# The low half of the MLP weights: ScalarE's negated copy and two adding transfers in place of GpSimd's subtraction

## The reference, cut to what matters

```
def _sqrelu_mlp(h, w1, w2):
    u = jax.nn.relu(h @ w1)
    return (u * u) @ w2

def second_block(...):
    for i in range(DEPTH_2):
        hn = _rmsnorm(h, mix_norm_g[i])
        ...
        h = h + _sqrelu_mlp(_rmsnorm(h, mlp_norm_g[i]), mlp_w1[i], mlp_w2[i])
    return _rmsnorm(h, final_norm_g)
```

## Time and profile before

| | us |
|---|---|
| median of the 2 runs shown | 1996.18 (1995.83 to 1996.54) |
| span of the profiled execution, first to last instruction | 1992.5 |
| PE busy in it | 1975.0 |
| GpSimd busy in it | 915.7 |
| ScalarE busy in it | 782.6 |
| VectorE busy in it | 974.1 |

### The profile page before, as it was taken

The page is one execution under the profiler, slowest core; times in us unless marked ns, Lnnn a source line. Parts: engine busy times, 40 slices in busy tenths (PEclk is TensorE's granted clock), DMA queues, the critical chain, the costliest instruction groups (busy, mean ns, idle before and its releaser), DMA issues.

```text
span 1992.5 us, 24116 instructions
## 1 busy us (share of the span) xinstructions
PE 1975.0 (99%) x9360; PEld 1640.7 (82%) x9360; DVE 974.1 (49%) x1447; ACT 782.6 (39%) x1137; POOL 915.7 (46%) x662
## 2 busy tenths in 40 slices
PE   8999999999999999999999999999999999999998
PEld 7877878888888888888888888888888888888887
DVE  7667753432358745454555131325466783132234
ACT  7546442321235443434354132233455553223232
POOL 2433555545455344444445454545333345454552
PEclk9999999999999999999999999999999999999999
DMA  5312367375322313232323323233222223323231
GB/s 162 93 49 69 116 94 123 88 101 114 100 90 85 127 64 106 65 104 68 101 66 103 100 90 106 84 105 105 84 84 85 94 74 106 106 85 105 92 98 64
DMA packets 165555, 187.05 MB, mean 94 GB/s; under 512 B 3992, under 2 KB 152224, under 8 KB 165344
## 3 DMA queue, kind: packets, MB, share of 16 engines
q1 hardware_dynamic: 163632, 181.61, 28.6%
q10 hardware_dynamic: 1584, 3.74, 4.2%
q0 software_dynamic: 256, 0.55, 0.1%
HBM read 180.77 MB, written 4.72 MB: 93 GB/s over the span
## 4 chain that ended last, share of the span: by engine, by line
PE 92%; DVE 3%; issue 2%; ACT 1%; POOL 1%; DMA 1%; DVEq 0%; SPq 0%; POOLq 0%; ACTq 0%
PE ps L729 29%; PE ps L730 29%; PE ps L731 29%; PE ps L931 1%; PE ps L901 1%; POOL w_lo L654 1%; PE ps L940 1%; PE ps L941 1%; PE ps L918 1%; ACT w_hi L1338 0%; DMA freq<-in_c_freq 0%; DVE hn_lo L2481 0%; DVE x L2476 0%; DVE scr L1983 0%; ACT scr L1540 0%
## 5 line engine op out<-in xcount | busy, mean ns | idle before, releaser
L654 POOL TENSOR_TENSOR w_lo<-raw,w_hi 128x512 fp32r<-128x512 f32 x636 | 897.1, 1442 | 989.1 <-ACT w_hi L1338 989.1
L729 PE MATMUL ps<-hn_hi,w_hi 128*128 128x512 f32 x1524 | 600.4, 394 | 2.3 <-DVE hn_lo L2328 1.7
L1338 ACT ACTIVATE w_hi<-raw 128x2048 fp32r<-128x2048 f32 (+1 forms) x162 | 308.9, 1907 | 735.5 <-PE ps L731 735.4
L730 PE MATMUL ps<-hn_lo,w_hi 128*128 128x512 f32 x1524 | 593.4, 389 | 0.0
L731 PE MATMUL ps<-hn_hi,w_lo 128*128 128x512 f32 x1524 | 593.4, 389 | 0.0
L730 PE MATMUL ps<-hid_lo,w_hi 128*128 128x512 f32 x904 | 351.7, 389 | 0.0
L729 PE MATMUL ps<-hid_hi,w_hi 128*128 128x512 f32 x888 | 347.0, 391 | 0.1
L731 PE MATMUL ps<-hid_hi,w_lo 128*128 128x512 f32 x888 | 345.6, 389 | 0.0
L729 PEld LDWEIGHTS ps<-hn_hi,w_hi 128*128 128x128 f32 x1524 | 286.2, 188 | 67.4 <-issue 3.5
L731 PEld LDWEIGHTS ps<-hn_hi,w_lo 128*128 128x128 f32 x1524 | 286.1, 188 | 60.4
L730 PEld LDWEIGHTS ps<-hn_lo,w_hi 128*128 128x128 f32 x1524 | 286.3, 188 | 58.9 <-issue 1.4
(11 more groups left out here) (322 smaller groups left out, 1882.9 us busy)
## 6 DMA issues: line engine op xcount, KB each, us to landing
raw<-in_mlp_w SPq DMA_DIRECT2D x64, 1024.0 KB, 5.3
raw<-in_ret_w_in SPq DMA_DIRECT2D x24, 1024.0 KB, 5.1
raw<-in_att_w_in SPq DMA_DIRECT2D x12, 1024.0 KB, 5.2
raw<-in_w_gate SPq DMA_DIRECT2D x11, 1024.0 KB, 5.4
raw<-in_w_up SPq DMA_DIRECT2D x11, 1024.0 KB, 5.3
raw<-in_w_down SPq DMA_DIRECT2D x8, 1024.0 KB, 8.0
raw<-in_ret_w_out SPq DMA_DIRECT2D x8, 1024.0 KB, 5.1
raw<-in_w_in SPq DMA_DIRECT2D x7, 1024.0 KB, 5.7
```

What stands on the lines that cost most here:

```text
L654: ins = pool.tensor_tensor(w_lo[:, slot, at], raw[:, slot, at], w_hi[:, slot, at].bitcast(F32), ALU.subtract)
L729: pe.matmul(o, hi, rhs_hi, start=start, stop=False, skip_group_check=True)
L730: pe.matmul(o, hi, rhs_lo, start=False, stop=False, skip_group_check=True)
L1338: act.activation(w_hi[:, c.slot, 0:columns], raw[:, c.slot, 0:columns], ACT.Copy)\
```

## The change

Of the 64 MLP chunks all but the first of each MLP, 2 x 31 = 62, get their low half in another way. ACT writes -raw, rounded to float32r, into `w_lo` in two halves of 1024 columns (`neg_ready` counts each half), and only then copies raw to `w_hi`. POOL issues, for each half as it is ready, a DMA that reads the same weights from DRAM once more and adds them to what stands in `w_lo` (`accum_op=ALU.add`); then it waits for `w_hi_ready` and for both transfers, and counts `w_lo_ready` up by an empty instruction. The first chunk of each MLP and all other chunks keep GpSimd's subtraction. SP, PE and DVE do what they did.

To have three semaphores more (`neg_ready`, `lo_first_in`, `lo_second_in`), the twelve of the first attention's head pairs and those of the second's are made one set, with a count that runs on from the first to the second (`nth`). The waits are on the same events as before.

```diff
+BY_DMA = MLP_A.chunks * MLP_A.iters - 1
+def dma_index(ph, number):
+    return number - ph.chunk0 - 1 + (BY_DMA if ph is MLP_B else 0)
...
-                return s[f"{self.name}_{what}"]
+                return s[f"pair_{what}"]
...
-            first = RET.chunk0 + 2
-            after = (N_CHUNKS - first) // 2
-            with pool.Fori(0, after) as i:
-                lo(first + 2 * i, first % 2)
-                lo(first + 1 + 2 * i, (first + 1) % 2)
-            for c in range(first + 2 * after, N_CHUNKS):
-                lo(c, c % 2)
+            def lo_run(first, end):
+                after = (end - first) // 2
+                with pool.Fori(0, after) as i:
+                    lo(first + 2 * i, first % 2)
+                    lo(first + 1 + 2 * i, (first + 1) % 2)
+                for c in range(first + 2 * after, end):
+                    lo(c, c % 2)
+            def lo_added(n, slot, number, src):
+                halves = ((slice(0, 1024), s["lo_first_in"]), (slice(1024, 2048), s["lo_second_in"]))
+                for half, (at, landed) in enumerate(halves):
+                    pool.wait_ge(s["neg_ready"], 2 * n + half + 1)
+                    dst = w_lo[:, slot, at].rearrange("p (k c) -> p k c", k=4)
+                    pool.dma_start(dst, src[:, 4 * half:4 * half + 4, :], accum_op=ALU.add).then_inc(landed, 16)
+                pool.wait_ge(s["w_hi_ready"], number + 1)
+                for _at, landed in halves:
+                    pool.wait_ge(landed, 16 * n + 16)
+                pool.nop().then_inc(s["w_lo_ready"], 1)
+            def lo_added_run(ph, layer):
+                w1 = T["mlp_w1_2"][layer].rearrange("(k p) (g m c) -> g m p k c", p=P, m=4, c=256)
+                w2 = T["mlp_w2_2"][layer].rearrange("(g k p) (m c) -> g m p k c", p=P, k=8, c=256)
+                first = ph.chunk0 + 1
+                n = dma_index(ph, first)
+                pool.wait_ge(s["w_lo_ready"], first)
+                for m in range(BY_DMA):
+                    i, j = divmod(m + 1, 8)
+                    lo_added(n + m, (first + m) % 2, first + m, w1[i, j] if j < 4 else w2[i, j - 4])
+            lo_run(RET.chunk0 + 2, MLP_A.chunk0 + 1)
+            lo_added_run(MLP_A, 0)
+            lo_run(ATT.chunk0, MLP_B.chunk0 + 1)
+            lo_added_run(MLP_B, 1)
...
+            def split_negated(ph, c):
+                act.wait_ge(raw_ready[c.slot], c.loads)
+                act.wait_ge(s["group_done"], c.two_before)
+                for half in range(2):
+                    at = slice(1024 * half, 1024 * half + 1024)
+                    act.activation(w_lo[:, c.slot, at], raw[:, c.slot, at], ACT.Copy, scale=-1.0)\
+                        .then_inc(s["neg_ready"], 1)
+                act.activation(w_hi[:, c.slot, :], raw[:, c.slot, :], ACT.Copy).then_inc(s["w_hi_ready"], 1)
...
-                split(following)
+                split_negated(ph, ph.chunk(1))
...
-                        split(ph.chunk(m + 2, i))
+                        split_negated(ph, ph.chunk(m + 2, i))
...
-                        split(ph.chunk(6 + m, i))
+                        split_negated(ph, ph.chunk(6 + m, i))
...
-                    if following and m < 3:
+                    if following and m < 2:
+                        split_negated(ph, following)
+                    if following and m == 2:
                         split(following)
```

More of the change, by code:

```diff
@@ L208 @@
  ret_v_mean ret_v_lo ret_sq ret_acc ret_var ret_ln ret_rstd ret_ys ret_gate ret_y ret_y_hi ret_y_lo
- two_s two_mx two_nmx two_exp two_rs two_p two_t two_hi two_lo two_pv two_shift two_o two_ohi two_olo
+ two_ohi two_olo
  gain_pair ffn_old_hi ffn_old_lo apart_done apart_scaled apart_sum gate_old_hi gate_old_lo gate_old_done gate_e_hi gate_e_lo gate_sig gate_read
- mlp_sq mlp_hi mlp_lo att_in_hi att_in_lo tab_scaled ffn_silu ffn_part fin_tmp fin_t fin_half fin_left fin_right""".split()
+ neg_ready lo_first_in lo_second_in mlp_sq mlp_hi mlp_lo att_in_hi att_in_lo tab_scaled ffn_silu ffn_part fin_tmp fin_t fin_half fin_left fin_right""".split()
 def build(nc, T, out):
@@ L391, in build @@
         class OnePair(Pair):
-            name, scale, negated = "one", DQ ** -0.5, (5, 8)
+            scale, negated = DQ ** -0.5, (5, 8)
             def qk(self, b):
@@ L425, in build @@
         class TwoPair(Pair):
-            name, negated = "two", (7, 8)
+            negated = (7, 8)
             def __init__(self, p):
                 self.p, self.group, self.half = p, p // 2, p % 2
+                self.nth = ONE_PAIRS + p
                 self.slot = 8 * (self.group % 2)
@@ L909, in pair_scores_by_kind @@
                 if p:
-                    pe.wait_ge(a.sem("o"), 2 * p)
-                pe.wait_ge(a.sem("mx"), 8 * p + 2)
+                    pe.wait_ge(a.sem("o"), 2 * a.nth)
+                pe.wait_ge(a.sem("mx"), 8 * a.nth + 2)
                 for nth in range(2):
@@ L1383, in gained_hi, with gained_x @@
                 act.activation(hn_hi[:, t, :], x[:, t, :], ACT.Copy, scale=gain(*at)).then_inc(s["norm_hi"], 1)
-            def gained_x(norm, adding, name, row, following):
+            def gained_x(norm, adding, name, row, ph):
                 for t in range(KD):
@@ L1545, in pair_prob_hi @@
                 if a.p or b:
-                    act.wait_ge(a.sem("pv"), 2 * a.p + b)
+                    act.wait_ge(a.sem("pv"), 2 * a.nth + b)
                 for j, done in T_ORDER[b]:
-                    act.wait_ge(a.sem("t"), 8 * a.p + 4 * b + done)
+                    act.wait_ge(a.sem("t"), 8 * a.nth + 4 * b + done)
                     act.activation(a.pt(0, j), a.trans_ps(b, j), ACT.Copy).then_inc(a.sem("hi"), 1)
             def pair_shift(a, b):
-                act.wait_ge(a.sem("pv"), 2 * a.p + b + 1)
+                act.wait_ge(a.sem("pv"), 2 * a.nth + b + 1)
                 if a.p:
-                    act.wait_ge(a.sem("o"), 2 * a.p - 1 + b)
+                    act.wait_ge(a.sem("o"), 2 * a.nth - 1 + b)
                 here, there = a.rows(b), a.rows(1 - b)
@@ L1598, in _ @@
             conv_hi(1)
[L1599 removed]
+            act.wait_ge(s["pair_t"], 8 * ONE_PAIRS)
             for t in range(2):
@@ L1891, in mlp @@
                         split(following)
-            gained_x(N_MLPA, [RET.group(n, RH - 1) for n in range(6, 10)], "mlp_norm_g_2", 0, MLP_A.chunk(1))
+            gained_x(N_MLPA, [RET.group(n, RH - 1) for n in range(6, 10)], "mlp_norm_g_2", 0, MLP_A)
             mlp(MLP_A, N_MLPA, 0, N_ATT, ("mix_norm_g_2", 8))
@@ L1963, in _ @@
             next_split(52)
-            gained_x(N_MLPB, [ATT.group(ATT.groups - n) for n in (4, 3, 2, 1)], "mlp_norm_g_2", 8, MLP_B.chunk(1))
+            gained_x(N_MLPB, [ATT.group(ATT.groups - n) for n in (4, 3, 2, 1)], "mlp_norm_g_2", 8, MLP_B)
             mlp(MLP_B, N_MLPB, MLP_GROUPS * 8, N_FINAL, None)
@@ L2204, in pair_negated @@
             def pair_negated(a, b):
-                dve.wait_ge(a.sem("mx"), 8 * a.p + a.negated[b])
+                dve.wait_ge(a.sem("mx"), 8 * a.nth + a.negated[b])
                 four = slice(4 * b, 4 * b + 4)
@@ L2223, in pair_prob_lo @@
                 for j, done in T_ORDER[b]:
-                    dve.wait_ge(a.sem("hi"), 8 * a.p + 4 * b + done)
+                    dve.wait_ge(a.sem("hi"), 8 * a.nth + 4 * b + done)
                     dve.tensor_tensor(a.pt(1, j), a.trans_ps(b, j), a.pt(0, j).bitcast(F32), ALU.subtract)\
```

38 lines of the change are left out of this document (19 added, 19 removed).

## The result

The changed kernel takes 2021.57 us (2020.61 to 2022.53, 2 runs) for 1996.18 before: a ratio of 1.0127, 95% interval 1.011 to 1.0144. It is slower, as forecast, but by 25 us and not by the 62 us that the prediction put on it, and inside 2%. The range, 1993 to 2270, held it; the size was missed by more than half, and "slower by over 2%", which had most of the chance, did not come.

A forecast was written before the change was run, and what follows sets the result against it. PE was taken as the bound, with at most 1 us to win; the profiled span of 1992.5 us plus 63 us of late chunks minus 1 gave 2054.5, and 3.7 around it 2058 us; range 1993 to 2270.

The forecast's parts named there:

- PE as the bound, and nothing to win: Whole kernel: PE busy 1975.0 of 1992.5 us, so freeing POOL and DVE gains at most 1 us in all.
- A = 6.6: DMA engines: us to move a chunk's two adding halves, 1 MB, taken as two passes against 3.3 for a plain load.
- Cost nothing: ACT: two negated halves add 2.1 us a chunk, but squares, high copies and MLP heads still come in time.
- POOL's own part: POOL's issue of each adding transfer: 0.89 us an instruction, the time of its own DMA instruction in the trace.
- The collision of the load with the adding bytes: MLP chunks: the next plain load and the next chunk's adding transfers share the DMA engines unless 1.5 us of reserve remain.
- the sum A + 5.3: Period of late chunks, ready to ready: adding bytes' time plus fixed costs and load; 11.9 us against PE's 10.9.
- above that each chunk eats the reserve of the next: MLP chunks: with adding bytes over 5.6 us, one chunk's lateness delays the load that collides with the next; POOL ends as bound.
- 62 x 1.0: All 62 chunks by DMA: each loses 1.0 us, 63 us in all.
- The threshold of A = 5.6: MLP chunks: adding bytes under 5.6 us miss the load's bytes and nothing stalls, about 1996 us.
- 3.8 + 6.6: Time from a chunk's start to its readiness: 3.8 us fixed plus the adding bytes, before what the next load's bytes take.
- Rival 4: PE, once it stalls a tenth of the time, gets a lower clock; no share, as early slices less busy had 1.00.
- The 3.7 us: Time around the profiled span, added to 2054.5 us to stand beside the runs' median, giving 2058.

The follow-up runs named there:

- the run with half the load: Changed kernel, but SP's plain load of an MLP chunk brings only its first 512 KB, both adding transfers whole: 2005.34 us, ratio 1.0048.
- the run with one transfer: Changed kernel with one adding transfer of 1 MB a chunk, issued after both negated halves, in place of two of 512 KB: 2031.99 us, ratio 1.0185.
- quarters: Changed kernel with four negated quarters and four adding transfers of 256 KB a chunk in place of two halves: 2069.86 us, ratio 1.0372.
- the loop written out: Changed kernel with PE's loop over each MLP's middle rounds written out, same instructions in the same order: 2029.76 us, ratio 1.0174.

## Why the prediction was right or wrong

- PE as the bound, and nothing to win: right. POOL and DVE were freed of 189 and 77 us, and no kernel of the study beat 1995 by more than noise.
- The price of adding, A = 6.6: right, 6.7 us on the engines, and about 6.1 from first byte to last for a chunk in time. The Trainium skill, page "Collectives: The Full Stack", section "The bandwidth ceiling: the fold count and why AG ≠ RS ≠ AR", has the half rate, measured there for collectives, that gave the estimate of 6.4; against SP's loads (3.3 us) the trace agrees with it, against a copy from the same queue (4.4 us) it is only 1.5 times.
- ScalarE: 1.05 us a half, as worked out, and the MLPs' `hid_lo` never late. "Cost nothing" was wrong for the heads of the MLPs by 3 us: I had looked at the sums behind that split and not at the chunk that the split itself makes.
- POOL's own part: 1.3 and 1.6 us an instruction for the 0.9 taken from a plain small transfer. Small, but it eats from the reserve.
- The collision of the load with the adding bytes: right as a mechanism; the run with half the load shows that it is what keeps chunks late. For the chunks deepest in it the step is 11.9 to 12.2 us, as the sum A + 5.3 had it.
- The failed step is the one after it: "above that each chunk eats the reserve of the next", up to "62 x 1.0". It took the regime in which a collision is full for that of every chunk. Two things were wrong in it. The threshold of A = 5.6 asked for no overlap at all of load and adding bytes. The time to readiness had been right, 3.8 + 6.6 = 10.4 us; measured, a chunk whose turn came at 1343.56 was ready at 1353.80, 10.2 us, with the load's tail (to 1348.0) running over its first adding bytes (from 1347.2). The next turn came at 1354.46, so half a microsecond was to spare, and this repeats for twelve chunks at a stretch. And a chunk that is late without a collision is paid only every second time, as the run with one transfer shows. In place of 62 chunks at 1.0 us there are 32 at 0.78.
- What decides between the regimes was not in the prediction: packets of the instruction queue of 1 us. It had thought of code only as POOL's new code, at a microsecond or two in all; the packets are those of PE's code, which is the same as before. They pass unseen in the kernel before (six of them in its 1060 to 1230 us), because there they can only hold up a load, and a load had time: the one issued at 1109.25 lands some 5.3 us later, and its split starts at 1123.8.
- Rival 4, a lower clock for PE, got no share. For the profiled run of the changed kernel that is right: the clock was 1.00 from 9.8 us to 2016.8 us. But the reason given was too thin. Where PE waited longer at a stretch the clock did fall, in the kernels with half the load (3.1 us) and with quarters (2.9 to 5.1 us).
- The 3.7 us for what lies around the span were too much: the runs have 1.8 to 2.0 us (2022.53 for a span of 2020.7). The sum would have been 2056 in place of 2058.

## What to carry to other kernels

The work-ahead chain that just fits had two regimes here, and its cost was not the mean length of the chain but the share of time in which small disturbances had pushed it over. So compare the reserve left with the longest single disturbance in the trace (here a 16 KB instruction packet of about 1 us), and keep more than that: three quarters of the moved bytes cost 1.7 us, all of them 26 to 29. And before moving work from an idle engine to the DMA queues, ask what bounds the kernel: here each engine that was freed had been free enough.

## What the runs showed of the hardware

- An adding DMA from DRAM into SBUF, in rows of 1 KB on POOL's queue, took 102 ns a packet on its DMA engine, a copying one 66 ns, a load on SP's queue 56 ns (28.1% of 16 x 2020.7 us over 163632 packets). Adding bytes moved at 195 GB/s, loads at up to 388.
- The same transfer cost POOL 0.74 us as a copy and 1.28 us or more as an addition.
- Code fetching disturbs data transfers: one 16 KB packet of q8 takes about 1.1 us on one DMA engine, and an adding transfer beside it landed about that much later (9.5 to 10.1 us after POOL's start for 8.4 to 8.8, in seven cases of seven). PE's loop body of three packets was fetched once and not again in its later iterations.
- PE's granted clock fell to 0.50 for 3.4 to 6.8 us after each of the six waits of 3.7 to 5.1 us in the kernel with quarters. After waits of 2.8 to 3.2 us it went either way: it fell after 3.1 us with half the load and stayed at 1.00 after 3.2 us with the loop written out.
